# Attention values with standing weights, turned by transposes; norm factor and masks on GpSimd

## What is computed

```python
a = rms_norm(h, norm_mix)                       # h: (1, 272, 1024)
q, k, v, ... = split_cols(a @ w_in)             # q, k, v: 512 columns each
s_win  = where(in_win, q k_window^T * 64**-0.5 + bias[rpb], -1e30)
s_meta = q k_meta^T * 64**-0.5
p = softmax(concatenate([s_win, s_meta]))
o_grid = p_win @ v_window + p_meta @ v_meta
```

## Time and profile before

| | |
|---|---|
| median of three runs | 818.51 us |
| profiled execution: span, first to last instruction | 817.8 us (the page gives no other time of its own; the median stands 0.7 us above this span) |
| busy: TensorE / VectorE / ScalarE / GpSimd | 98% / 79% / 61% / 15% |
| chain of waits that ended last, share by engine | TensorE 92%, VectorE 4%, ScalarE, DMA and GpSimd 1% each |
| granted TensorE clock, mean over the span | 0.997 |
| DMA, mean over the span | 208 GB/s |

### The profile page before, as it was taken

The page is one execution under the profiler, slowest core; times in us unless marked ns, Lnnn a source line. Parts: engine busy times, 40 slices in busy tenths (PEclk is TensorE's granted clock), DMA queues, the critical chain, the costliest instruction groups (busy, mean ns, idle before and its releaser), DMA issues.

```text
span 817.8 us, 17229 instructions
## 1 busy us (share of the span) xinstructions
PE 803.5 (98%) x6996; PEld 787.0 (96%) x6996; DVE 643.0 (79%) x1022; ACT 497.9 (61%) x891; POOL 123.8 (15%) x137
## 2 busy tenths in 40 slices
PE   6999999999999999999999999999999999999996
PEld 6999999989999999999999999999999999999996
DVE  7788599977987878786998898887987568566673
ACT  6575566756677465655666744555676457566652
POOL 0022255401040000000240620001203130000001
PEclk9999999999999999999999999999999999999998
DMA  9934544466667989898777567675765336455441
GB/s 337 382 96 140 165 142 122 154 195 205 194 201 235 355 304 342 305 324 331 249 249 252 164 208 219 216 260 179 207 180 167 127 122 189 177 155 156 149 130 53
DMA packets 47022, 170.42 MB, mean 208 GB/s; under 512 B 5216, under 2 KB 5472, under 8 KB 46688
## 3 DMA queue, kind: packets, MB, share of 16 engines
q1 hardware_dynamic: 46224, 165.31, 61.8%
q10 hardware_dynamic: 720, 4.01, 1.2%
HBM read 168.26 MB, written 1.05 MB: 207 GB/s over the span
## 4 chain that ended last, share of the span: by engine, by line
PE 92%; DVE 4%; ACT 1%; DMA 1%; POOL 1%; issue 0%; SPq 0%; POOLq 0%; DVEq 0%; ACTq 0%
PE bank L196 91%; DVE wl L235 2%; DMA raw<-in_ws 1%; POOL sq L235 1%; DVE raw L223 0%; PE bank L199 0%; ACT wh L205 0%; SPq L193 0%; ACT sq L202 0%; DVE B0l L223 0%; DVE h L223 0%; DVE B1l L235 0%; ACT B1h L202 0%; ACT B0h L202 0%; DVE gd L235 0%
## 5 line engine op out<-in xcount | busy, mean ns | idle before, releaser
L235 DVE TENSOR_TENSOR wl<-raw,wh 128x1024 fp32r<-128x1024 f32 (+1 forms) x260 | 327.6, 1273 | 22.6 <-ACT wh L205 21.5
L205 ACT CAST wh<-raw 128x1024 fp32r<-128x1024 f32 (+1 forms) x260 | 269.0, 1046 | 105.2 <-DMA raw<-in_ws 53.7
L196 PE MATMUL bank<-XAh,wl 128*128 128x256 f32 (+1 forms) x896 | 254.7, 284 | 0.1
L196 PE MATMUL bank<-XAl,wh 128*128 128x256 f32 (+1 forms) x896 | 249.0, 278 | 0.0
L196 PE MATMUL bank<-XAh,wh 128*128 128x256 f32 (+1 forms) x896 | 248.8, 278 | 0.0
L196 PEld LDWEIGHTS bank<-XAh,wl 128*128 128x128 f32 x896 | 168.4, 188 | 3.1 <-issue 1.3
L196 PEld LDWEIGHTS bank<-XAh,wh 128*128 128x128 f32 x896 | 168.6, 188 | 0.1
L196 PEld LDWEIGHTS bank<-XAl,wh 128*128 128x128 f32 x896 | 168.6, 188 | 0.0
L196 PE MATMUL bank<-B1h,wl 128*128 128x256 f32 (+1 forms) x464 | 129.3, 279 | 0.0
L196 PE MATMUL bank<-B1l,wh 128*128 128x256 f32 (+1 forms) x464 | 128.7, 277 | 0.0
L196 PE MATMUL bank<-B1h,wh 128*128 128x256 f32 (+1 forms) x464 | 128.6, 277 | 0.0
(11 more groups left out here) (276 smaller groups left out, 1219.6 us busy)
## 6 DMA issues: line engine op xcount, KB each, us to landing
raw<-in_ws SPq DMA_DIRECT2D x306, 512.0 KB, 4.5
bias<-in_bias ACTq DMA_DIRECT2D x1, 1664.0 KB, 12.0
hK<-in_xk SPq DMA_DIRECT2D x4, 272.0 KB, 5.4
h<-in_xt ACTq DMA_DIRECT2D x1, 1088.0 KB, 7.4
out<-gd SPq DMA_DIRECT2D x4, 256.0 KB, 2.6
raw<-in_ws SPq DMA_DIRECT2D x2, 256.0 KB, 3.9
C<-in_cst SPq DMA_DIRECT2D x1, 512.0 KB, 8.5
crow<-in_crow ACTq DMA_DIRECT2D x1, 512.0 KB, 6.0
```

The source lines that it names most:

```text
L196: return self.real.matmul(*a, **k)
L205: return self.real.copy(*a, **k)
L235: return self.real.tensor_tensor(*a, **k)
```

## The change

The values are made as the keys are: units of 256 columns with the weights standing, 272 tokens streaming, 24 matmuls of 272 columns per unit. ScalarE copies each of four tiles from PSUM to `vT` (which lies in `gna`, unused until later), GpSimd multiplies it by `rsK` (`v_scaled`), and TensorE transposes 128, 128 and 112 columns of it (`v_turn`) as one more stage of the side work, once per pair of heads. ScalarE copies the result to `vN` and `vM`. The matmuls and copy of `rcol` go; a pad takes its place in SBUF. The masks move from VectorE to GpSimd, in another order: three ahead of everything, then mask(s + 2) right behind shares(s).

By the order of the yields v_turn(0) comes right behind turn(1), v_turn(1) behind turn(3), v_turn(2) behind turn(5), and v_turn(3) directly ahead of pv(3), behind `qh`'s second unit. On ScalarE the copies of tiles 2 and 3 come behind exp(2); on GpSimd v_scaled of tiles 2 and 3 comes ahead of shares(2).

```diff
-    mat("w_in", 1024, 1536, w=512)
+    mat("w_in", 1024, 1536)
...
+        vT = bass.AP(gna[:, :, :].tensor, gna[:, :, :].offset, [list(gna[:, :, :].ap[0]), [272, 4], [1, 272]])
...
 # TensorE, attention()
                     if 2 <= s <= 9:
-
-                        if s % 2:
-                            p = s // 2 - 1
+                        p = s // 2 - 1
+                        if s % 2 == 0:
+                            ps = side.take("v_turn", p)
+                            e.wait_ge(*at("v_scaled", p))
+                            e.transpose(ps[:, 0:128], vT[:, p, 0:128], cst_("ident"))
+                            e.transpose(ps[:, 128:256], vT[:, p, 144:272], cst_("ident"))
+                            e.transpose(ps[0:112, 256:384], vT[:, p, 64:176], cst_("ident")).then_inc(*up("v_turn", p))
+                            side.give(("v_turn", p), ("v", p))
+                        else:
                             ps = side.take("pv", p)
                             e.wait_ge(*at("turned", 2 * p))
                             e.wait_ge(*at("turned", 2 * p + 1))
-                            e.wait_ge(*at("v", (0, 2)))
+                            e.wait_ge(*at("v", p))
...
-            ps = side.take("rcol")
-            e.wait_ge(*at("rs", "mix"))
-            for b, t in enumerate((0, 144, 64)):
-                m = e.matmul(ps[:, 2 * b:2 * b + 2], rsK[:, t:t + 128], cst_("ident", 2), start=True, stop=True)
...
-            t_rows("v", "w_in", 1024, 1536, XU, unnormed("mix"), lambda b, col: [("v", (col, b))],
-                   ((0, 128), (144, 272), (64, 176)))
+            t_tiles("v", "w_in", 1024, 1536, XU, unnormed("mix"), lambda t: [("v_raw", t)], n1=272)
 # ScalarE
+                        p = s // 2 - 1
+                        if s % 2 == 0:
+                            ps, n = bk("v_turn", p), slice(128 * p, 128 * p + 128)
+                            e.wait_ge(*at("v_turn", p))
+                            e.copy(vN[:, :, n], in_halves(ps[:, 0:256]))
+                            e.copy(vM[:, n], ps[0:112, 256:384]).then_inc(*up("v", p))
...
-            e.wait_ge(*at("rcol_turn", 0))
-            e.copy(rcol[:, :], bk("rcol")[:, 0:6]).then_inc(*up("rcol", 0))
-            rows("v", "w_in", 1024, 1536, v_out)
+            tiles("v", "w_in", 1024, 1536, to("v", lambda t: vT[:, t, :], "v_raw", lambda t: t, n=272))
 # VectorE: mask(0), mask(s + 1) and their definition go
 # GpSimd, attention()
+                mask(0)
+                mask(1)
                 for s in range(10):
                     if s < 8:
                         if s == 1:
                             shares(0)
+                        if s == 0:
+                            mask(2)
                         yield
                     if 1 <= s <= 8:
                         if s < 8:
                             shares(s)
+                        if s < 6:
+                            mask(s + 2)
                         yield
...
+            def v_scaled(ts):
+                for t in ts:
+                    e.wait_ge(*at("v_raw", t))
+                    e.tensor_tensor(vT[:, t, :], vT[:, t, :], rsK[:, 0:272], ALU.mult).then_inc(*up("v_scaled", t))
...
-            rows("v", "w_in", 1024, 1536)
+            tiles("v", "w_in", 1024, 1536, v_scaled)
```

More of the change, by code:

```diff
@@ L412, in build @@
         PTm = [sbt(pna, f"PTm{i}", [112, 256]) for i in range(2)] + [sq3[0:112, 0:256]]
-        rcol = sbt(pna, "rcol", [128, 6])
+        sbt(pna, "sPpad", [128, 8])
+        vT = bass.AP(gna[:, :, :].tensor, gna[:, :, :].offset, [list(gna[:, :, :].ap[0]), [272, 4], [1, 272]])
         nmr = [sbt(pna, f"nm{i}", [128, 6]) for i in range(3)]
@@ L524, in build @@
         AT_ONCE = ("mlp", "even", "fin", "odd")
-        ALONE = ("k", "oo2", "zf", "a", "qk", "glr")
+        ALONE = ("k", "v", "oo2", "zf", "a", "qk", "glr")
         def tile(label, t, n=256):
@@ L570, in streams @@
             return any(name == n and c0 <= col < c1 for n, c0, c1 in (
-                ("w_in", 1024, 1536), ("w_in", 3072, 3584), ("even_in", 2048, 3072), ("odd_in", 1024, 2048),
+                ("w_in", 3072, 3584), ("even_in", 2048, 3072), ("odd_in", 1024, 2048),
                 ("odd_in", 4112, 5136)))
@@ L924, in tensor_program @@
             w.steps = 2
-            ps = side.take("rcol")
-            e.wait_ge(*at("rs", "mix"))
-            for b, t in enumerate((0, 144, 64)):
-                m = e.matmul(ps[:, 2 * b:2 * b + 2], rsK[:, t:t + 128], cst_("ident", 2), start=True, stop=True)
-            m.then_inc(*up("rcol_turn", 0))
-            side.give(("rcol",), ("rcol", 0))
-            t_rows("v", "w_in", 1024, 1536, XU, unnormed("mix"), lambda b, col: [("v", (col, b))],
-                   ((0, 128), (144, 272), (64, 176)))
+            t_tiles("v", "w_in", 1024, 1536, XU, unnormed("mix"), lambda t: [("v_raw", t)], n1=272)
             w.steps = 2
@@ L1442, in attention @@
                         yield
[L1444 to L1449, removed]
             def meta_rows(label, N, M):
@@ L2140, in attention @@
             def attention():
[L2141 to L2144, removed]
                 def share(hh):
@@ L2160, in score @@
                                     negate=True).then_inc(*up("most", hh))
-                mask(0)
                 for s in range(10):
-                    if s < 7:
-                        mask(s + 1)
                     if s < 8:
@@ L2190, in vector_program @@
             w.steps = 2
-            rows("v", "w_in", 1024, 1536)
+            tiles("v", "w_in", 1024, 1536, nothing)
             def gates(label, d, f_, k_):
@@ L2739, in shares, with mask @@
                         *up("prob", hh))
+                def mask(hh):
+                    e.wait_ge(one["bias"], 16)
+                    e.wait_ge(one["negw"], 16)
+                    e.tensor_tensor(bias[:, hh, :], bias[:, hh, :], negw[:, :], ALU.add).then_inc(*up("bias", hh))
+                mask(0)
+                mask(1)
                 for s in range(10):
```

## The result

| | before | after |
|---|---|---|
| median, us | 818.76 (4 runs) | 824.01 (4 runs, 822.11 to 825.45) |
| ratio to before, 95% interval | | 1.0063 [1.0049, 1.0077] |
| profiled span, us | 817.8 | 821.8 |
| granted TensorE clock, mean | 0.997 | 0.994 |

The change costs 5.2 us, 0.63%. The forecast was +2.3 us, 820.8 in a range of 816.0 to 823.3: the direction is right, the time lies outside. The profiled execution took 823.63 us, 1.8 more than its span.

A forecast was written before the change was run, and what follows sets the result against it. TensorE bounds the kernel, the softmax chain over VectorE, ScalarE and GpSimd a second limit hidden by under a microsecond. +0.5 (turn(2)) + 0.6 + 1.2 = +2.3 on span 817.8 gives 820.1, plus 0.7: 820.8 us, range 816.0 to 823.3.

The forecast's parts named there:

- TensorE's own work, -5.8 and +1.2: Values' phase: matmuls and rcol shrink from 17.9 to 12.1 us, gaining 5.8; four groups of added transposes cost 1.2.
- v_turn(3) ahead of pv(3), 0.9 us: TensorE stalls 0.9 us ahead of pv(3), waiting for ACT's copies of v_turn(3); bounds 0.6 and 2.
- The chain to turn(0): Early masks on POOL hold VectorE's small operations, +1.15 us; moved masks give back 1.5; TensorE waits 3.4 us at turn(0).
- the larger figure (2.6 us for three masks): Chain to turn(0): each early mask costs VectorE 0.88 us rather than 0.62; the forecast would be about 1 us higher.
- a granted clock under 1.00: Sign of a wrong forecast: TensorE's clock falls behind the waits, making it slower by something not in the sum.
- The chain to turn(2): score(2) at 53.9, prob(2) 6.65 us later at 60.55; TensorE waits 2.5 us, starting turn(2) 0.5 us later than before.
- Behind it, +1.8: After turn(2) nothing is regained: v_turn(1) and (2) cost 0.6 us, v_turn(3) with its stall 1.2.
- From span to time: The median stands 0.7 us above the profiled span: 820.1 becomes 820.8 us.
- (a): Rival: the softmax chain does not hold TensorE, collisions fall in VectorE's gaps; -3.7 us, 814.8; chance 0.15.
- (b): Rival: waits at turn(0) and turn(2) but mild collisions, turn(2) at about 58.5; sum 0, 818.5 us; chance 0.25.
- (c): Rival: masks last 1.78 us each, mask(1) late for score(1); turn(2)'s chain 1.5 to 3 us worse; 823; chance 0.12.

The follow-up runs named there:

- e8: The change with the edits of e2, e4, e6 and e7 together, and v_turn(3) with its copies one step earlier: 816.01 us, ratio 0.9962.
- e5: The kernel before with only the masks moved to GpSimd, in the change's order: 819.36 us, ratio 1.0002.
- e7: The change with VectorE's small operations moved, some ahead of the queries, the rest behind the values: 819.52 us, ratio 1.0008.
- e3: The change with the edits of e1 and e2 together: 819.48 us, ratio 1.0008.
- e2: The change, but VectorE applies the values' factor from PSUM; ScalarE's four copies and GpSimd's v_scaled go: 820.91 us, ratio 1.0025.
- e4: The change with the masks back on VectorE in the order of before: 822.34 us, ratio 1.0040.
- e1: The change with 34 dummy matmuls ahead of TensorE's wait at turn(0), to keep its clock up: 824.49 us, ratio 1.0063.
- e9: The kernel before with only VectorE's small operations moved as in e7: 819.26 us, ratio 1.0000.
- e11: e8 with VectorE's small operations back in their old place: 818.89 us, ratio 0.9992.
- e6: The change with turn(0) moved behind scores(2,3), one unit of values later: 823.52 us, ratio 1.0053.

## Why the prediction was wrong, point by point

The mechanism stood: TensorE waited at turn(0) and pv(3) for what the forecast named, and at turn(2) the chain of the other engines ended last, though by 0.2 us instead of 2.5. Two terms of the sum were too small, the masks' hold on VectorE's small operations (1.15 us, measured 2.2) and the offset from span to time (0.7, measured 1.8), and the fall of the clock had no price at all.

- **TensorE's own work, -5.8 and +1.2: right.** Units of 3.0 us, TensorE at turn(0) by 43.6; e8 brings the gain out but for 0.5 us.
- **v_turn(3) ahead of pv(3), 0.9 us: right**, measured 0.72. e8, which moves it, has no such wait.
- **The chain to turn(0), masks holding VectorE's small operations: the term that was mis-sized.** The forecast had +1.15 us (its own terms, 0.2 + 0.6 + 0.6 - 0.3, make 1.1), measured were +2.2 (`wl` at 38.48 instead of 36.18, less the 0.08 by which this execution began later). It took the mask's price from a hold of 0.6 and let 0.3 of idle pay for part. The three masks ran back to back, 1.05 us apart; they held one small operation each, by 0.56, 0.90 and 0.77 us, and the 0.3 of idle stayed. So share(0) came at 45.87, not 44.7, and turn(0) at 47.94, not 46.8: the 1.15 us is missing one to one. Of the rule in the Trainium skill, SBUF — State Buffer, section Who interferes with whom, that the blocked engine waits out the other's whole instruction, the forecast kept the larger figure (2.6 us for three masks) out of its sum. The trace agrees with that rule: each of the three ended 0.02 us behind the mask that it met, and so lost what was left of that mask, 2.2 us in all. e5 and e7 show the hold with other operations in its way.
- **What follows turn(0): a term that was left out.** The forecast named a granted clock under 1.00 only among what would make it wrong, and had no price for it. Unit 4 took 5.45 us instead of 3.0, and turn(0) 0.77 instead of 0.36. This alone moved TensorE's arrival at turn(2) by 2.9; prob(2), at 62.20, hid it. e3 against e2 shows what e2's shorter fall is worth when nothing hides it: (1.0025 - 1.0008) x 818.5 = 1.4 us.
- **The chain to turn(2).** From score(2) to prob(2) 6.65 us were forecast, 62.20 - 55.38 = 6.82 measured: right, collision by collision. Its start was wrong: score(2) at 55.38 instead of 53.9, 1.15 of it the masks' hold carried on; the other 0.3 came between share(0) and score(2), where an `XAl` that takes 0.44 us alone took 1.31, a hold of 0.87 where the forecast had 0.5 (another `XAl` and a `vt`, 0.49 alone, took 1.00 each, about as forecast). So turn(2) is 2.19 late, not 0.5.
- **Behind it, +1.8: right**, 4.26 - 2.19 = 2.07 measured.
- **From span to time.** The median is 3.2 us above the forecast. 1.7 of them are the later turn(2) (2.19 less 0.5): the span is 821.8, not 820.1. 1.1 are the offset between an execution's span and its time, the second term that was mis-sized: the forecast took 0.7 us, from one execution's span and a median over others; measured it is 823.63 - 821.8 = 1.8, and 1.75 to 1.94 in each execution of the kernel before beside the experiments. The other 0.4 lie between this execution and the median. So the profiled execution of before took about 819.6 us, at the upper end of its runs, which is why 5.2 us between the medians are only 4.0 between the spans.
- **What differs from execution to execution.** The profiles locate a microsecond of this kind. Behind 486 us the kernels are the same, yet three units of weights took 9.83 us in the change's profiled execution and 9.54 in e4's:

```profile
487.82 0.61 PE L196 MATMUL bank<-wT,vn 128*128 128x128 f32 x4
...
497.65 0.61 PE L196 MATMUL bank<-wT,vn 128*128 128x128 f32 x4
```

```profile
487.50 0.60 PE L196 MATMUL bank<-wT,vn 128*128 128x128 f32 x4
...
497.04 0.60 PE L196 MATMUL bank<-wT,vn 128*128 128x128 f32 x4
```

The granted clock is 1.00 in both. To 522 us this makes 1.15 us, which e1, e2 and e4 have less than the kernel before, the change and all other experiments; e1 has 1.7 more between 200 and 260 us. So up to a microsecond between two medians need not come from the edit.
- **Against the rivals.** (a) had no waits at turn(0) and turn(2): excluded by the waits above. (b) needed mild collisions; the kernels nearest to it are e3 and e7, 819.5. (c) had the masks at 1.78 each and 823, nearest to the measured time, but by luck: score(0) did not wait for a mask; the small operations were the ones held.

Left open: the masks' price inside the change. It is 0.6 us in the table and 1.9 by the ratios; 1.15 of the difference lies behind 486 us, where no mask is, and whether e4's edit has any part in it is not shown. Four executions of the change had spans from 820.3 to 823.7 us, at mean clocks from 0.994 to 0.997. Why the clock fell with waits of 2.9, 3.6, 3.7 and 4.35 us and not with 2.0, 2.55 and 2.85 was not tried.

## What to carry to other kernels

Before an engine's work is shortened, look how soon behind it the next chain of the others ends: with 0.77 and 0.53 us of margin, 5.8 us less on TensorE could bring only what that chain gave, and the same edit to the chain that gave nothing alone (e9) gave 1.9 once TensorE had been made faster (e8 against e11). Price moved work by where it lands: three operations on GpSimd cost VectorE 2.2 of their 3.2 us although it had only short operations there, and the kernel nothing where TensorE is the later one (e5). Of two limits that end together one can show as no gain when removed alone (e1) and be worth 1.4 us when the other goes (e3 against e2); test them together.

## What the runs showed of the hardware

- Three GpSimd operations of about 1.05 us in a row stretched one VectorE operation on 8 columns from 0.17 to 0.95 us and a pair from 0.24 to 0.85 (`lbw` in e5). In the change three operations of 0.16 us lost 0.56, 0.90 and 0.77 us, each to one mask, in e7 a `vt` of 0.49 us 0.83: being short did not make the hold short.
- GpSimd pays as well: the three masks took 3.16 us against small operations and 4.34 against `wl` and `vt`; two `v_scaled` 1.52 us in e7 where they met little, 3.38 against a `wl` pair.
- With a TensorE wait of 4.35 us the granted clock was 0.50 from 46.9, inside the wait, to 53.7; with one of 3.63 (e4) from 46.3 to 53.1; with one of 3.74 (e2) from 48.0 to 51.4; with one of 2.91 (e6) from 56.6 to 60.0. With waits of 2.0 (e7), 2.55 (e11) and 2.85 us (turn(2) in e1) it stayed at 1.00, and so it did with a wait filled with matmuls (e1). The waits of 2.85 and 2.91 us went different ways, and the one of 3.63 cost more than that of 3.74, so the length of the wait alone doesn't decide it.
- At a granted clock of 1.00 the same matmuls came 3% farther apart in some executions than in others, for stretches of 35 us and more (9.83 and 9.54 us for three units).
- Groups of four transposes took 0.36 us at clock 1.00, as in the earlier trace rows, and 47.94 to 48.71 = 0.77 at the lower one.
